# Seven half-size block products in place of eight in the last FFN's up projection, and the split of `a` put after it

## What is computed

```python
def swiglu(x, w_gate, w_up, w_down):
    return (jax.nn.silu(x @ w_gate) * (x @ w_up)) @ w_down
...
        h = rms_norm(x, ffn2_norm[l])
        x = x + FFN_RESIDUAL_WEIGHT * swiglu(h, ffn2_w_gate[l], ffn2_w_up[l], ffn2_w_down[l])
    return rms_norm(x, final_norm)
```

## Time and profile before

| | us |
|---|---|
| median of 3 runs | 2158.53 |
| lowest and highest | 2158.13, 2160.07 |
| span of the profiled execution | 2156.5 |
| PE busy in it | 2136.0 (99%) |
| DVE, ACT, POOL busy | 901.6, 889.2, 898.7 |

### The profile page before, as it was taken

The page is one execution under the profiler, slowest core; times in us unless marked ns, Lnnn a source line. Parts: engine busy times, 40 slices in busy tenths (PEclk is TensorE's granted clock), DMA queues, the critical chain, the costliest instruction groups (busy, mean ns, idle before and its releaser), DMA issues.

```text
span 2156.5 us, 27195 instructions
## 1 busy us (share of the span) xinstructions
PE 2136.0 (99%) x10936; PEld 1756.1 (81%) x10936; DVE 901.6 (42%) x1625; ACT 889.2 (41%) x1491; POOL 898.7 (42%) x383
## 2 busy tenths in 40 slices
PE   9999999999999999999999999999999999999998
PEld 8788877787888888888888888778888888888886
DVE  7684555436655401553332133644644132333211
ACT  7835555544544422442222232752356233222321
POOL 4423322345544543564444443143524444444431
PEclk9999999999999999999999999999999999999999
DMA  5313321332333332233333333123332333333321
GB/s 178 98 50 112 116 61 50 114 102 78 109 97 97 110 105 78 88 88 98 98 98 108 89 97 93 31 89 99 108 88 69 97 90 103 95 96 98 104 91 49
DMA packets 56429, 200.55 MB, mean 93 GB/s; under 512 B 6640, under 2 KB 7536, under 8 KB 55920
## 3 DMA queue, kind: packets, MB, share of 16 engines
q1 hardware_dynamic: 52416, 188.77, 29.1%
q10 hardware_dynamic: 3888, 10.05, 1.4%
HBM read 194.60 MB, written 2.10 MB: 91 GB/s over the span
## 4 chain that ended last, share of the span: by engine, by line
PE 95%; DVE 3%; ACT 2%; issue 1%; POOL 0%; ACTq 0%; DVEq 0%
PE dense L852 16%; PE dense L850 16%; PE dense L851 16%; PE misc L850 6%; PE misc L852 6%; PE misc L851 6%; PE misc L781 3%; PE misc L783 2%; PE misc L782 2%; PE dense L834 2%; PE dense L824 1%; PE dense L827 1%; PE dense L781 1%; PE dense L783 1%; PE dense L782 1%; PE dense L1224 1%
## 5 line engine op out<-in xcount | busy, mean ns | idle before, releaser
L703 POOL TENSOR_TENSOR w_lo<-raw,w_hi 128x1024 fp32r<-128x1024 f32 x349 | 853.5, 2459 | 1137.3 <-ACT w_hi L1514 1109.5
L1514 ACT ACTIVATE w_hi<-raw 128x1024 fp32r<-128x1024 f32 x352 | 362.5, 1051 | 147.0 <-PE dense L852 84.5
L850 PE MATMUL dense<-u_hi,w_hi 128*128 128x512 f32 x800 | 312.0, 390 | 0.0
L852 PE MATMUL dense<-u_hi,w_lo 128*128 128x512 f32 x800 | 311.3, 389 | 0.0
L851 PE MATMUL dense<-u_lo,w_hi 128*128 128x512 f32 x776 | 301.9, 389 | 0.0
L850 PE MATMUL dense<-a_hi,w_hi 128*128 128x512 f32 x528 | 206.2, 391 | 0.0
L852 PE MATMUL dense<-a_hi,w_lo 128*128 128x512 f32 x528 | 205.4, 389 | 0.0
L851 PE MATMUL dense<-a_lo,w_hi 128*128 128x512 f32 x528 | 205.4, 389 | 0.0
L850 PE MATMUL misc<-u_hi,w_hi 128*128 128x512 f32 x464 | 180.8, 390 | 0.0
L852 PE MATMUL misc<-u_hi,w_lo 128*128 128x512 f32 x464 | 180.5, 389 | 0.0
L851 PE MATMUL misc<-u_lo,w_hi 128*128 128x512 f32 x456 | 177.5, 389 | 0.0
(11 more groups left out here) (501 smaller groups left out, 3793.7 us busy)
## 6 DMA issues: line engine op xcount, KB each, us to landing
raw<-in_weights SPq DMA_DIRECT2D x352, 512.0 KB, 3.6
h<-in_x SPq DMA_DIRECT2D x4, 512.0 KB, 6.7
alibi<-in_alibi ACTq DMA_DIRECT2D x1, 2048.0 KB, 8.6
...
```

The lines of the kernel that those rows point to most:

```text
L703: nc.gpsimd.tensor_tensor(w_lo[:, s % SPLITS, :, :], raw[:, s % RAWS, :, :], w_hi[:, s % SPLITS, :, :].bitcast(F32), ALU.subtract).then_in ...
L850: mm(out, hi, src_hi[:, i, :], start=(i == 0), stop=False)
L852: last = mm(out, lo, src_hi[:, i, :], start=False, stop=(i == k - 1))
L1514: f(w_hi[:, s % SPLITS, :, :], raw[:, s % RAWS, :, :], ACT.Copy).then_inc(w_part, 1)
```

## The change

For `up2`, chunk pairs 0 to 3 stay as they were. From pair 4 on (`PAIRED`: pairs 4 to 21, 18 of them, numbered p = 0 to 17) the product of a pair is seen as a 2x2 block product: tokens in two halves of 256, K in two halves of 4 tiles, outputs in gate and value. Instead of eight block products (half the tokens, half of K, one output) seven are computed, of sums and differences of blocks (Strassen's form, in Winograd's variant):

- Each product is 4 K steps of 3 matmuls of 128x256. A pair has 84 matmuls of 256 columns where it had 48 of 512.
- The sums of `u` (`s_all`, four of 128x1024) and their split (`s_hi` on ACT, `s_lo` on DVE) are made once. Since these are of `u` with r in it, `u` is rewritten in mid-layer (`rewrite_sums` on DVE, `rewrite_hi(..., sums=True)` on ACT), and chunk 4 waits for the new `u_lo` (`again=8 * DC`). From pair 2 on no output is multiplied by `r_sb`.
- The differences of weights are made per pair from the two raw slabs: three on DVE (into PSUM, `misc[2]`, `misc[3]`), one on POOL (`t_three`). Each of the seven 128x512 weight blocks is rounded on ACT and its low part made on POOL (four) or DVE (three).
- PE's products add up in three banks x, y, z (`pair_banks`). ACT copies x after the first product (`st_first`), DVE makes five sums from the banks (`st_out` 1 to 5), ACT takes silu in two halves, DVE multiplies. PE waits for `st_first` before product 3, for `st_out` 1 before product 4, 2 before product 6 and 3 before product 7.
- `s_hi` and `s_lo` lie where `a_lo` of the later tiles belongs. So tiles 5 to 20 of a are kept whole (`a_kept`, in the place of `a_hi`), and only after the last pair is each split: ACT rounds it into `a_lo`'s place, DVE subtracts into `a_hi`'s, and `down2` reads the two swapped (`turned_from`). ACT rounds a slab of `down2` after every fourth of them.

The two attention stages also share their semaphores now, with offsets; that moves no instruction.

```diff
+            def paired(name):
+                first, second = slice(0, 256), slice(256, S)
+                blocks = {"a11": (u_hi[:, 0:4, first], u_lo[:, 0:4, first]),
+                          "a12": (u_hi[:, 4:8, first], u_lo[:, 4:8, first]),
+                          "a22": (u_hi[:, 4:8, second], u_lo[:, 4:8, second])}
+                blocks.update({f"s{i + 1}": (s_hi[:, i, :, :], s_lo[:, i, :, :]) for i in range(4)})
+                def product(p, i, out, a, start):
+                    hi, lo = piece(w_hi, p, i), piece(w_lo, p, i)
+                    a_h, a_l = blocks[a]
+                    for k in range(4):
+                        mm(out, hi[:, k, :], a_h[:, k, :], start=(start and k == 0), stop=False, skip_group_check=True)
+                        mm(out, hi[:, k, :], a_l[:, k, :], start=False, stop=False, skip_group_check=True)
+                        last = mm(out, lo[:, k, :], a_h[:, k, :], start=False, stop=(k == 3), skip_group_check=True)
+                    last.then_inc(st_used, 1)
...
+                    product(p, 0, x, "a11", True)
...
+                    product(p, 1, y, "s2", True)
+                    pe.wait_ge(st_pool, 5 * p + 3)
+                    pe.wait_ge(st_first, p + 1)
+                    product(p, 2, x, "a12", False)
+                    pe.wait_ge(st_pool, 5 * p + 4)
+                    pe.wait_ge(st_out, 5 * p + 1)
+                    product(p, 3, y, "s3", False)
...
+                    product(p, 4, z, "s1", True)
+                    pe.wait_ge(st_lo, 3 * p + 2)
+                    pe.wait_ge(st_out, 5 * p + 2)
+                    product(p, 5, y, "a22", False)
+                    pe.wait_ge(st_pool, 5 * p + 5)
+                    pe.wait_ge(st_out, 5 * p + 3)
+                    product(p, 6, z, "s4", False)
...
-            dense("up2", u_hi, u_lo, (u_ready, 7 * DC), row="pre4", row_at=(0, 2))
-            dense("down2", a_hi, a_lo, (a_ready, 2 * FC), row="pre5", row_at=(DC - 1, FC - 2))
+            dense("up2", u_hi, u_lo, (u_ready, 7 * DC), row="pre4", row_at=(0, 2), again=8 * DC, upto=8)
+            paired("up2")
+            dense("down2", a_hi, a_lo, (a_ready, 2 * FC), row="pre5", row_at=(DC - 1, FC - 2), turned_from=KEPT_FROM)
...
+                    act.wait_ge(st_used, BLOCKS * (PAIR_NO[(name, paired_to - 1)] + 1))
+                    for c in range(KEPT_FROM, FC - 1):
+                        act.wait_ge(a_raw, FC * n + c + 1)
+                        f(a_lo[:, c, :], a_kept[:, c, :], ACT.Copy).then_inc(a_part, 1)
+                        if c % 4 == 0:
+                            feed_to(rounded[0] + 1)
...
+                for c in range(KEPT_FROM, FC - 1):
+                    dve.wait_ge(a_part, FC * n + c + 1)
+                    TT(a_hi[:, c, :], a_kept[:, c, :], a_lo[:, c, :].bitcast(F32), ALU.subtract).then_inc(a_ready, 1)
```

More of the change, by code:

```diff
@@ L110, with first_slab, hi_no, diff_no @@
 NSLABS = -(-TILES // SLAB)
+PAIRED = {"up2": (4, FC)}
+PAIRS = [(name, c) for name, (lo, hi) in PAIRED.items() for c in range(lo, hi)]
+LAYER_OF = {"up": 0, "up1": 1, "up2": 2}
+BLOCKS = 7
+def first_slab(name, c):
+    return START[name][0] // SLAB + 2 * c
+PAIR_AT = {first_slab(*pair) + i: (p, i) for p, pair in enumerate(PAIRS) for i in range(2)}
+PAIR_NO = {pair: p for p, pair in enumerate(PAIRS)}
+def hi_no(p, i):
+    return 4 * (list(PAIRED).index(PAIRS[p][0]) + 1) + BLOCKS * p + i
+def diff_no(p, i):
+    return 4 * (list(PAIRED).index(PAIRS[p][0]) + 1) + 3 * p + i
+def sum_no(name, i, each):
+    return 4 * list(PAIRED).index(name) + each * PAIR_NO[(name, PAIRED[name][0])] + i
+def ring_plan():
+    half_of, block_of, half = {}, {}, 0
+    for s in range(NSLABS):
+        if s not in PAIR_AT:
+            assert half % 2 == 0
+            half_of[s] = half
+            half += 2
+        elif PAIR_AT[s][1] == 0:
+            block_of[PAIR_AT[s][0]] = half
+            half += BLOCKS
+    return half_of, block_of
+HALF_OF, BLOCK_OF = ring_plan()
+def plain_before(s):
+    return sum(d not in PAIR_AT for d in range(s))
 DIAG = (0, 512, 1024, 896)
@@ L833, in dense @@
                             s, j = divmod(before, SLAB)
-                            last = mm(out, w_hi[:, s % SPLITS, j, :], src_lo[:, i - 1, :], start=False, stop=(i == k))
+                            last = mm(out, w_hi[:, ring(s), j, :], src_lo[:, i - 1, :], start=False, stop=(i == k))
                             used(last, before)
@@ L838, in dense @@
                     tile += ahead * k
-                for m in range(ahead, n):
+                for m in range(ahead, upto or n):
                     g = g0 + m
@@ L2163, in _ @@
             late_act(4, 32, "ffn2", "up2", "out")
-            ffn_swiglu(2, "up2")
+            rewrite_hi(2 * DC + 4, "up2", 2 * (DC - 2), [u_all[:, c, :] for c in range(DC)], sums=True)
+            ffn_swiglu(2, "up2", *PAIRED["up2"])
             norm_act(5, 40, "down2")
```

440 lines of the change are left out of this document (368 added, 72 removed).

## The result

The changed kernel takes 2173.16 us (median of 4 runs, 2172.12 to 2173.75) against 2158.33 before: a ratio of 1.0068, 95% interval 1.0054 to 1.0082. That is 14.8 us slower; I had forecast 2168.4, and 2152.5 to 2173.0 as the range, so the direction was right and the median lies 0.2 us above the range (the four runs of one kernel differ by more, 1.6 us). The profiled execution took 2173.03 us, its span is 2171.2, 14.7 more than before.

What follows compares the result with a forecast made beforehand. PE was taken as the bound, busy 2136.0 of 2156.5 us. Terms −14.4 + 4.5 + 1.6 + 11.2 + 7.0 gave +9.9: span 2166.4, and 2168.4 us with the runs' median 2.0 above; range 2152.5 to 2173.

Steps and rivals of the forecast that it cites:

- the clock's: PE's clock may fall to 1.2 GHz during the wait of item 1: 0 to 3 us in the ranges.
- item 1: Rewrite of u before chunk 4 of up2: PE waits for u_lo behind sums and POOL's lock, +4.5 us, bounds 3 to 7.
- item 4: Split of a at the start of down2: POOL's slab operations hold up DVE's subtractions, +7.0 us, bounds 4 to 8.5.
- the forecast case: Whole kernel: POOL wins the lock in the pairs and all four delays occur, 2163 to 2172 us, chance 0.43.
- the case where all goes wrong: Pairs lose 1.0 us each and the clock falls twice: up to 2176 us; above 2172 got 0.10.
- PE's own work: Paired chunks of up2: 84 starts at 0.120 us make 10.08 in place of 10.88, −14.4 us for 18 pairs.
- Item 2: First pair in up2: DVE's work queued ahead of L2678 makes PE wait, +1.6 us, bounds 0 and 3.
- Item 3: Pairs in full swing: L2663 loses the lock to POOL, product 4 is 0.7 us late, 16 pairs, +11.2 us or nothing.
- the tie: In each pair DVE's L2663 and POOL's low part want the lock within 0.09 us; POOL wins by a little.
- the 0.14 us "that POOL needs to take hold": Lock in the pairs: reason given for POOL winning, as this time must be shared with DVE's own start.
- the other outcome: DVE wins the lock in the pairs: −1.3 us, 2157.2; DVE wins or mixed, 2155 to 2163, chance 0.33.
- The exclusive lock: DVE operations with two SBUF inputs wait while POOL works: about 2.1 us per 128x1024 operation, 1.1 per 128x512.

Runs made afterwards that it cites:

- The runs with one fill and with both: Changed kernel, unread matmuls in PE's waits: before up2's chunk 4 (plus 21 behind down2's waits), 2170.52 us; before down2's tiles 10, 12, 13, 2170.52; both, 2168.08.
- experiment 6: Changed kernel with POOL's second low part of each pair made on 128 of its 512 elements: 2159.63 us, one run.
- Experiment 4: Changed kernel with DVE's product of the pair before (L2663) moved behind the sum PE waits for (L2678): 2162.88 us.
- experiment 5: Changed kernel with DVE's second weight difference of each later pair (L2592) made on 384 of its 512 elements: 2161.57 us.
- Experiment 7: Changed kernel with ACT rounding one slab of down2 within the split of a in place of four, the next ones near its end: 2164.04 us.
- experiments 2: Changed kernel with 7 unread matmuls each ahead of the waits for tiles 10, 12 and 13 of down2: 2170.52 us.

## Why the prediction was wrong

**The step that failed is the clock's.** The prediction says: "A fall to 1.2 GHz during the wait of item 1 is possible; each us of PE's work at that level costs one more, and I allow 0 to 3 us for it in the ranges", and its sum has 0 for it. The clock fell twice. The first fall cost 2.3 us, the second, behind the waits of item 4 where I had not looked for one, 2.75. The runs with one fill and with both (2170.52 twice, 2168.08) take 2.64 us off each, and 5.1 together. The row that spoke for it was on the table: in the earlier trace rows the clock is at half 3.4 us after PE's last matmul at 2147.1, and my own wait for item 1 was 4.5 us long. By my numbers the fall belonged in the forecast case: at some 2.5 us a place the sum would have been about 2173.4. The same omission made the range too short above, since I had left two falls to the case where all goes wrong, with a small share of 0.10. How far outside the range the time came to lie was chance: with stretches at half clock of 3.4 us, as in experiment 6, it would have been some 2 us lower and inside, and the term of 0 just as wrong.

The rest of the sum, term by term (span):

| term | predicted | measured |
|---|---|---|
| PE's own work, 18 pairs | -14.4 | -14.4 (84 starts in 10.08 us) |
| phase at the start of `up2` | 0 | -0.3 |
| 1. rewrite of u | +4.5 | +4.0 |
| 2. first pair | +1.6 | +2.1 |
| 3. pairs in full swing | +11.2 | +11.0 (16 x 0.69) |
| 4. split of a | +7.0 | +6.8 |
| clock | 0 | +5.1 (2.3 and 2.75) |
| sum | +9.9 | +14.3; the spans differ by 14.7 |

- **PE's own work**: right, and the rows decided between two numbers. The formula of the Trainium skill (TensorE: Matmul & The Clock Gate, Back-to-back issue gap), which the page calls the gap of an isolated matmul, would give 0.109 us for 256 columns; the trace has 0.120, as the earlier trace rows had.
- **Item 1**: the mechanism and POOL's four operations in DVE's way as forecast; `u_lo` began at 1809.0 and not 1809.7. (The 4.0 is 3.9 and the restart.)
- **Item 2**: bigger by 0.5 and put together otherwise: two waits, each for a sum behind an operation that lost to POOL, where I had one.
- **Item 3**: the tie was called with 0.09 us between the two and was 0.11. POOL won as forecast, 0.69 us a pair. It was luck in part: the experiment with 0.14 us less on DVE turns it over, so 11 us of this result hung on something that my durations, good to 0.1 us, could not decide. Experiment 4 has DVE losing at 0.05 us behind, so a lag of 0.09 did mean that POOL wins; I had no row between 0.02 and 0.18, and the reason I gave, the 0.14 us "that POOL needs to take hold", is not shown: what the traces have is that POOL, when it is late, ends 1.16 us after DVE (experiment 5), which is 0.14 less than its 1.30. Keeping the other outcome as a rival at 0.33 was right.
- **Item 4**: POOL's four starts were forecast to 0.1 us, tile 13 at 15.7 us after the start and found at 15.6. Experiment 7 shows the cause.
- **The exclusive lock** stands as the earlier trace rows had it. On the pair of ports the Trainium skill (SBUF — State Buffer, two separate sides) agrees with experiments 4 to 7: a DVE operation with two SBUF inputs waits until POOL's operation is through (1.74 in place of 0.69 us), and one with an operand in PSUM does not (L2690 took 0.41 us from 1843.66 on in the changed kernel, inside an operation of POOL's from 1843.09 to 1844.37).

Of the 0.4 us between the sum and the spans 0.24 lies in pair 1, which takes 11.01 us and not 10.77: a second short gap, before product 6. What stays open is the rest of it, and what sets the moment of a fall and the length of a stretch at half clock. At chunk 4 it is 6.8 us in the changed kernel and in experiments 5 and 7, where the clock fell during the wait, and 3.4 in experiments 2, 4 and 6, where it fell 0.7 to 0.9 us after PE had begun again; in `down2` it was between 3.4 and 10.2, and with no such order.
